# mLSTM, LRU and SSD steps at other beats, head squares tile by tile on POOL, and a tenth place for gated tiles

## The chip, the cores and the metric

The kernel runs on one core of a Trainium2 chip. It computes four layers in one launch on a sequence of 256 positions, in fp32. The metric is the device time of one execution in microseconds. The engines are named as in the profile: PE is TensorE, DVE is VectorE, ACT is ScalarE, POOL is GpSimd and SP is SyncE.

## What is computed

The reference applies two layers of a first block (LRU with mLSTM, then SSD) and two layers of a second one (attention with spatial gating, then a gated feed-forward net). The change touches the first block. Cut to its core:

```python
def lru_mlstm_layer(x, ...):
    u = x @ w_in                                   # 2048 -> 8192
    x_l, x_m, z = jnp.split(u, [LRU_WIDTH, LRU_WIDTH + MLSTM_WIDTH], axis=-1)
    y_l = rglru(causal_conv(x_l, ...), ...)        # 16 blocks of 128
    x_mc = jax.nn.silu(causal_conv(x_m, ...))
    q, k, v, o = ...                               # per head, 4 heads of 512
    gates = (gin @ w_if + b_if)                    # input and forget gate rows
    h = mlstm_chunkwise(q, k, v, ig, lf)
    h = rmsnorm(h, m_norm)                         # per head: sum of squares over 512
    y_m = (o * h).reshape(bn, s, MLSTM_WIDTH)
    y = jnp.concatenate([y_l, y_m], axis=-1) * jax.nn.silu(z)
    return y @ w_out

def ssd_layer(x, ...):
    z, xbc, dt = jnp.split(x @ w_in, ...)
    xbc = jax.nn.silu(causal_conv(xbc, ...))       # xs, B, C
    cb = einsum(cm, bm)                            # per group, 8 groups
    y = ssd_scan(xh, dt, a, bm, cm) + d_skip * xh  # 8 heads of 64 in a group
    y = y * jax.nn.silu(z)
    y = rmsnorm(y per group, gnorm)                # sum of squares over 512
    return y @ w_out
```

## The kernel before

Activations stand transposed, 128 features by 256 positions in a tile. Each weight matrix is read in chunks of 128 x 1024 (512 KB) by SP into RAW; ACT rounds a chunk to its high part WH, DVE subtracts to get the low part WL (line 1266, in RAW's place), and PE multiplies each 128 x 128 block twice: WL with the activation's high half (line 522, 256 columns) and WH with both halves (lines 521 and 524, 512 columns). An output tile (a job) sums 4 to 32 such blocks in one of four psG banks; ACT copies one half of the bank (`half`), DVE adds the other and scales (`evict`).

`Schedule` lists all jobs and cuts the chunks into 2324 beats, half a chunk each: four blocks, eight matmuls. Everything else is tied to beats. Each engine's program is one loop over the beats, and in each beat it issues the steps whose event lies a fixed number of beats back, `for h in at("head", b - 21)`, in the order in which the functions are called. Engines run free of each other otherwise and wait on semaphores: PE loops over beats with `lstm`, `norms`, `ssd` ahead of the beat's blocks; ACT splits a chunk at each even beat, three chunks ahead of PE, and DVE at each odd beat. So a step at a later beat stands behind more of the engine's own work; it takes no other time by itself. Jobs end at fixed beats: z tile n at 116 + 4n for n > 0, LRU tile n at 184 + 8n, LRU gate tile n at 180 + 8n, an SSD group every 40 beats.

**mLSTM.** Event `gates` is at beat 119; before the change `head` h is at 128 + 16h. The gate rows are made by ACT and DVE (`gates`), PE turns them to columns (line 587), ACT stores them and reads them back broadcast to NMB. For a head PE makes K Q products (594), DVE and ACT the weights E, PE the denominator (600) and four tiles of numerators (607), DVE scales them to hs (1413). POOL sums their squares into hacc (hq in the profile; `squares`, lines 1740 to 1746), PE sums them over partitions (`colsum`, line 505, head + 21), ACT makes the root hr in two activations (781, 783), DVE gates and scales hs with z tiles (1420 to 1423, semaphore h_y), ACT writes the high half to Y (yh_hi) and DVE the low half (yh_lo). z tiles are gated by ACT (993) and POOL (`fma`, lines 1725 and 1727, shared tile SQ); nine places hold them until their head is finished.

**LRU.** POOL convolves a tile (1730, 1725, 1727), PE multiplies by two 128 x 128 weights (617, 618), ACT and DVE make the gates, DVE scans and multiplies by the gate, ACT and DVE write Y. The last layer output reads Y of LRU tile 15 in beat 329.

**SSD.** For a group: convolutions of B, C and four x tiles, the product CB (642, event `cb`), eight heads of decay weights Et made by DVE (1528), ACT (exp) and DVE (1535, 1536) and used by PE (660, head event + 5), outputs gated by z on POOL (1819), squares summed on POOL (event `gsum`) and by PE (line 505 from sq, event `gnorm`), root on ACT, four normalising steps on DVE (1548), high half to Y on ACT, low half on DVE (1271).

## Time and profile before

| | before |
|---|---|
| median of 3 runs | 3592.89 us (3592.19 to 3593.06) |
| profiled execution, its own time | 3593.61 us |
| its span | 3591.7 us |
| granted TensorE clock over it | 0.991 |
| PE busy | 97% |
| DVE busy | 76% |
| ACT busy | 53% |
| POOL busy | 47% |
| HBM read | 618.75 MB, 173 GB/s |

The span runs from the first to the last instruction of the program; the time has some 2 us around it. Matmuls are pipelined, so a busy PE is not PE at its peak. In a timeline row the number in brackets is the time that the engine stood idle before the row, and what ended it; short ones are not printed. PEclk is the share of the full TensorE clock that was granted: 1.00 is 2.4 GHz, 0.50 is 1.2 GHz. The mLSTM heads stand between 217 and 381 us, the LRU tiles until 565, SSD from 720 to 1305.

### The profile page before, as it was taken

The page shows a single profiled execution, that of the slowest core. Times are in us where ns is not written, and L with a number is a line of the kernel's source. Part 1 is how long each engine was busy: PE and PEld are TensorE (multiplying, and loading weights), DVE is VectorE, ACT ScalarE, POOL GpSimd, SP SyncE. Part 2 cuts the span into 40 slices and gives each one's busy share as a digit, 9 for nine tenths or more (in the row PEclk, how much of TensorE's full clock was granted, in tenths as well). Part 3 has the DMA queues.
Part 4 walks back from the last instruction along what each step waited for, and adds up shares of the span by engine and source line. Part 5 has one row for each costly group of instructions (what it writes and reads, how often), then busy time and mean ns, then how long its engine had stood idle before and what let it go on. Part 6 is the DMA issues. An engine that isn't in the chain of part 4 may idle for free.

```text
span 3591.7 us, 52952 instructions
## 1 busy us (share of the span) xinstructions
PE 3489.6 (97%) x19584; PEld 3001.1 (84%) x19584; DVE 2729.6 (76%) x4035; ACT 1891.9 (53%) x2857; POOL 1689.4 (47%) x1473
## 2 busy tenths in 40 slices
PE   8998999999999999998999999999998999999999
PEld 7887788888887888886888888888886888888888
DVE  8768886679899976776788758877676788658875
ACT  6554785455555554765444434444765544434443
POOL 4324672167877822143366406653143466306640
PEclk9999999999999999999999999999998999999999
DMA  5544556655555556543555665566543555665566
GB/s 192 168 156 140 162 182 186 188 180 170 176 169 166 178 165 188 178 132 111 186 188 187 184 189 187 186 185 188 173 134 110 186 188 187 184 191 185 187 185 179
DMA packets 177041, 624.37 MB, mean 174 GB/s; under 512 B 19784, under 2 KB 25616, under 8 KB 175760
## 3 DMA queue, kind: packets, MB, share of 16 engines
q1 hardware_dynamic: 171216, 606.11, 53.7%
q10 hardware_dynamic: 5568, 14.89, 1.2%
q8 instruction: 155, 2.54, 0.3%
q14 instruction: 102, 0.84, 0.1%
HBM read 618.75 MB, written 2.17 MB: 173 GB/s over the span
## 4 chain that ended last, share of the span: by engine, by line
PE 71%; DVE 10%; POOL 5%; ACT 3%; issue 3%; DMA 0%; ACTq 0%; POOLq 0%; DVEq 0%
PE psG L524 43%; PE psG L522 23%; DVE WL L1266 3%; PE psG L521 2%; POOL SQ L1725 1%; ACT WH L761 1%; DVE sdx L1279 1%; POOL SQ L1744 1%; ACT L781 1%; POOL sdx L1727 1%; PE psM L547 1%; DVE Et L1528 1%; DVE Et L1535 0%; POOL GV L1866 0%; DVE Y L1271 0%
## 5 line engine op out<-in xcount | busy, mean ns | idle before, releaser
L524 PE MATMUL psG<-H,WH 128*128 128x512 f32 x5655 | 2025.9, 398 | 0.0
L1266 DVE TENSOR_TENSOR WL<-RAW,WH 128x1024 fp32r<-128x1024 f32 (+1 forms) x1162 | 1496.0, 1287 | 552.7 <-ACT WH L761 550.8
L761 ACT ACTIVATE WH<-RAW 128x1024 fp32r<-128x1024 f32 (+1 forms) x1162 | 1214.8, 1045 | 952.3 <-PE psG L524 932.5
L522 PE MATMUL psG<-H,WL 128*128 128x256 f32 x6032 | 1667.2, 287 | 0.1
L524 PEld LDWEIGHTS psG<-H,WH 128*128 128x128 f32 x5655 | 1068.5, 189 | 234.1
L522 PEld LDWEIGHTS psG<-H,WL 128*128 128x128 f32 x6032 | 1146.1, 190 | 45.3 <-issue 9.6
L524 PE MATMUL psG<-Y,WH 128*128 128x512 f32 x2816 | 998.6, 398 | 0.0
L522 PE MATMUL psG<-Y,WL 128*128 128x256 f32 x2944 | 807.5, 281 | 11.6 <-DVE Y L1273 10.6
L524 PEld LDWEIGHTS psG<-Y,WH 128*128 128x128 f32 x2816 | 530.4, 188 | 122.1
L522 PEld LDWEIGHTS psG<-Y,WL 128*128 128x128 f32 x2944 | 557.0, 189 | 26.0 <-DVE WL L1266 11.2
L1875 POOL TENSOR_SCALAR fou<-fsu,PAR 128x256 f32<-128x256 f32 x88 | 177.9, 2022 | 565.3 <-DVE fsu L1308 565.3
L1787 POOL TENSOR_TENSOR SQ<-X 128x256 f32<-128x256 f32 x75 | 49.5, 661 | 358.4 <-DVE X L1319 358.4
L1725 POOL TENSOR_SCALAR SQ<-fsu,PAR 128x255 f32<-128x255 f32 x176 | 172.8, 982 | 16.9
L1727 POOL TENSOR_TENSOR fou<-SQ,fou 128x255 f32<-128x255 f32 x176 | 166.5, 946 | 14.7
L521 PE MATMUL psG<-H,WH 128*128 128x512 f32 x377 | 154.9, 411 | 13.1 <-DVE H L1273 11.8
L1883 POOL TENSOR_TENSOR fou<-fou,fog 128x256 f32<-128x256 f32 x88 | 133.4, 1515 | 6.9
L1839 POOL TENSOR_TENSOR g_t<-g_s 128x256 f32<-128x256 f32 x32 | 48.2, 1505 | 182.6 <-DVE g_s L1308 182.6
L1725 POOL TENSOR_SCALAR SQ<-sds,PAR 128x255 f32<-128x255 f32 (+2 forms) x96 | 120.0, 1250 | 9.3
L1790 POOL TENSOR_TENSOR SS<-SS,SQ 128x256 f32<-128x256 f32 x75 | 119.0, 1587 | 5.9
L761 ACT ACTIVATE fsu<-psG 128x256 f32<-128x256 f32 x88 | 33.9, 385 | 153.3 <-PE psG L524 153.3
L761 ACT ACTIVATE fsg<-psG 128x256 f32<-128x256 f32 x88 | 33.8, 384 | 151.3 <-PE psG L524 151.1
L1295 DVE TENSOR_TENSOR fsg<-psG,fsg 128x256 f32<-128x256 f32 x88 | 37.4, 425 | 78.6 <-ACT fsg L761 78.5
(350 smaller groups left out, 3578.9 us busy)
## 6 DMA issues: line engine op xcount, KB each, us to landing
RAW<-in_w_up SPq DMA_DIRECT2D x352, 512.0 KB, 3.6
RAW<-in_w_o_in SPq DMA_DIRECT2D x162, 512.0 KB, 3.6
RAW<-in_w_e_in SPq DMA_DIRECT2D x128, 512.0 KB, 3.6
RAW<-in_w_down SPq DMA_DIRECT2D x128, 512.0 KB, 3.5
RAW<-in_w_in SPq DMA_DIRECT2D x112, 512.0 KB, 3.6
RAW<-in_w_o SPq DMA_DIRECT2D x72, 512.0 KB, 3.6
RAW<-in_w_e_out SPq DMA_DIRECT2D x64, 512.0 KB, 4.3
RAW<-in_w_o_out SPq DMA_DIRECT2D x64, 512.0 KB, 4.2
```

Of the source, the lines that this page charges most:

```text
L521: e.matmul(o, wh, x, start=True, stop=False)
L522: ins = e.matmul(o[:, 0:T], wl, x[:, 0:T], start=False, stop=False, skip_group_check=True)
L524: ins = e.matmul(o, wh, x, start=False, stop=last)
L761: copy = lambda o, i, scale=1.0: e.activation(o, i, ACT.Copy, scale=scale)
L1266: tt(WL_[c % NRAW][:, 0:n], RAW_[c % NRAW][:, 0:n], WH_[c % NW][:, 0:n].bitcast(F32), SUB).then_inc(sem("wl"), 1)
L1725: own.up(ts(m, a, s, None, op0))
L1727: return tt(o, m, c, op1)
L1787: own.up(tt(sq, X[n], X[n], MUL))
L1790: step(tt(ss, ss, sq, ADD), "ssq")
L1839: own.up(tt(t, s, s, MUL))
L1875: own.up(ts(o, s, par(key, "fw", 88 + n), par(key, "fb", n), MUL, ADD))
L1883: step(tt(o, o, f_og[p % 2], MUL), "f_mul")
```

## The change

Events move: `head` by two beats, `cb` by two, `gsum` by one and `gnorm` by two for the first seven groups. Steps of `gates` on PE and ACT and the whole LRU chain from PE's product on move by two or three beats. The squares of a head are summed tile by tile, the first at head + 12 and each next a beat later, where all four stood at head + 15. z tiles get a tenth place, which lies where a row of the gates stood, so tile 9 waits for the gate rows, and the wait for h_y starts with tile 10. DVE's write of hs waits for yh_lo in place of yh_hi.

```diff
@@ -251,16 +251,16 @@
     for h in range(4):
-        S.event("head", h, S.events[("gates", 0)] + 9 + 16 * h)
+        S.event("head", h, S.events[("gates", 0)] + 11 + 16 * h)
...
         x3 = S.end_of("sx", g * 4 + 3)
-        S.event("cb", g, S.end_of("sC", g) + 14)
+        S.event("cb", g, S.end_of("sC", g) + 16)
...
             S.event("shead", g * 8 + e, x3 + 12 + (4 if g < 7 else 2) * e)
-        S.event("gsum", g, x3 + (48 if g < 7 else 34))
-        S.event("gnorm", g, x3 + (55 if g < 7 else 35))
+        S.event("gsum", g, x3 + (49 if g < 7 else 34))
+        S.event("gnorm", g, x3 + (57 if g < 7 else 35))
@@ -351,7 +351,7 @@
     gs, ig, gf, gz, gG, gM, gon = slots("gg", 7, 36)
-    zb = slots("zb", 2, 43) + slots("zb_", 1, 22) + slots("zx", 6, 23)
+    zb = slots("zb", 2, 43) + slots("zb_", 1, 22) + slots("zx", 6, 23) + slots("zy", 1, 42)
@@ -451,7 +451,7 @@
 
-    PLACE = {"xm": (xm_s, 3), "z": (zb, 9), "zl": (lz, 4), "lru": (ls, 2), "sz": (sd_z, 4), "V": (v2, 2),
+    PLACE = {"xm": (xm_s, 3), "z": (zb, 10), "zl": (lz, 4), "lru": (ls, 2), "sz": (sd_z, 4), "V": (v2, 2),
@@ -580,7 +580,7 @@
                 ready(use, ins)
-            for _ in at("gates", b - 7):
+            for _ in at("gates", b - 9):
@@ -608,9 +608,9 @@
             for h in at("head", b - 21):
-                w.wait_ge(sem("h_ssq"), h + 1)
+                w.wait_ge(sem("h_ssq"), 4 * h + 4)
                 colsum(("hc", h), hacc)
-            for n in at("lru", b - 10):
+            for n in at("lru", b - 12):
@@ -812,7 +812,10 @@
                 if n >= 9:
-                    w.wait_ge(sem("h_y"), n - 8)
+                    w.wait_ge(sem("gate_rows"), 1)
+                if n >= 10:
+                    w.wait_ge(sem("h_y"), n - 9)
@@ -945,11 +948,11 @@
                 e.activation(gz[0:4, :], gz[0:4, :], ACT.Ln, bias=KC[0:4, 3:4]).then_inc(sem("gate_soft"), 1)
-            for _ in at("gates", b - 5):
+            for _ in at("gates", b - 8):
...
                 e.dma_start(scr_m[1], gG[0:4, :]).then_inc(sem("st_m1"), 16)
-            for _ in at("gates", b - 8):
+            for _ in at("gates", b - 10):
@@ -990,7 +993,7 @@
                 w.wait_ge(sem("z_act"), n - 1) if n > 1 else None
-                e.activation(zt[n % 2], zb[n % 9], ACT.Tanh, scale=0.5).then_inc(sem("z_tanh"), 1)
+                e.activation(zt[n % 2], zb[n % 10], ACT.Tanh, scale=0.5).then_inc(sem("z_tanh"), 1)
@@ -1001,14 +1004,14 @@
                 e.dma_start(LW[n % 4], I["w_lru"][n]).then_inc(sem(f"lw{n % 4}"), 16)
-            for n in at("lru", b - 11):
+            for n in at("lru", b - 13):
...
                 e.activation(i, use.ap[:, T:2 * T], ACT.Tanh, bias=halves[:, 16 + n:17 + n], scale=0.5).then_inc(use.sem, 1)
-            for n in at("lru", b - 13):
+            for n in at("lru", b - 15):
@@ -1017,10 +1020,10 @@
                 e.activation(r, r, ACT.Ln, bias=one_c).then_inc(sem("l_ln"), 1)
-            for n in at("lru", b - 16):
+            for n in at("lru", b - 18):
...
                 e.activation(lr[n % 2], lr[n % 2], ACT.Exp, scale=0.5).then_inc(sem("l_exp"), 1)
-            for n in at("lru", b - 19):
+            for n in at("lru", b - 21):
@@ -1409,7 +1412,7 @@
                     w.wait_ge(sem("small"), use.done)
-                    w.wait_ge(sem("yh_hi"), 4 * (h - 1) + i + 1) if h else None
+                    w.wait_ge(sem("yh_lo"), 4 * (h - 1) + i + 1) if h else None
@@ -1417,10 +1420,10 @@
                     w.wait_ge(sem("o_tanh"), n + 1)
-                    stt(zb[n % 9], Og[n], 1.0, zb[n % 9], ADD, MUL)
+                    stt(zb[n % 10], Og[n], 1.0, zb[n % 10], ADD, MUL)
...
                     w.wait_ge(own.sem, own.n)
-                    tt(hs[i], hs[i], zb[n % 9], MUL).then_inc(sem("h_y"), 1)
+                    tt(hs[i], hs[i], zb[n % 10], MUL).then_inc(sem("h_y"), 1)
@@ -1431,15 +1434,15 @@
                 stt(lz[n % 4], lt[n % 2], 1.0, lz[n % 4], ADD, MUL).then_inc(sem("lz_act"), 1)
-            for n in at("lru", b - 12):
+            for n in at("lru", b - 14):
...
                 stt(xc, i, 1.0, xc, ADD, MUL).then_inc(sem("l_gate"), 1)
-            for n in at("lru", b - 15):
+            for n in at("lru", b - 17):
...
                 tt(lr[n % 2], ll2[n % 2], lr[n % 2], SUB).then_inc(sem("l_dif"), 1)
-            for n in at("lru", b - 17):
+            for n in at("lru", b - 19):
@@ -1448,7 +1451,7 @@
                 tt(l2, l2, lz[n % 4], MUL).then_inc(sem("l_scan"), 1)
-            for n in at("lru", b - 20):
+            for n in at("lru", b - 22):
@@ -1762,11 +1765,20 @@
                 w.wait_ge(sem("z_tanh"), n + 1)
-                step(fma(zb[n % 9], zt[n % 2], 1.0, zb[n % 9], ADD, MUL), "z_act")
-            for h in at("head", b - 15):
-                w.wait_ge(small[("pn", h, 3)].sem, small[("pn", h, 3)].out)
-                w.wait_ge(sem("small"), small[("hc", h - 1)].done) if h else None
-                squares(hacc, hs, "h_ssq")
+                step(fma(zb[n % 10], zt[n % 2], 1.0, zb[n % 10], ADD, MUL), "z_act")
+            for i in range(4):
+                for h in at("head", b - 12 - i):
+                    w.wait_ge(small[("pn", h, i)].sem, small[("pn", h, i)].out)
+                    if i == 0:
+                        w.wait_ge(sem("small"), small[("hc", h - 1)].done) if h else None
+                        step(tt(hacc, hs[0], hs[0], MUL), "h_ssq")
+                    else:
+                        sq_free()
+                        own.up(tt(sq, hs[i], hs[i], MUL))
+                        w.wait_ge(own.sem, own.n)
+                        w.wait_ge(sem("h_ssq"), 4 * h + i)
+                        step(tt(hacc, hacc, sq, ADD), "h_ssq")
```

The rows below are the programs of an engine as built, in issue order: line, operation, tiles and shape. The changed kernel has the same statements some lines further on. First POOL in the mLSTM stage, head 1, before and then changed; hs are the head's four tiles, hq the sum, SQ and zt, zb, zx, zy belong to the gating of z.

```order
L1725 TENSOR_SCALAR SQ<-zt_140 128x256
L1727 TENSOR_TENSOR zb_132<-SQ,zb_132 128x256
L1740 TENSOR_TENSOR hq_122<-hs_118 128x256
L1744 TENSOR_TENSOR SQ<-hs_119 128x256
L1746 TENSOR_TENSOR hq_122<-hq_122,SQ 128x256
L1744 TENSOR_TENSOR SQ<-hs_120 128x256
L1746 TENSOR_TENSOR hq_122<-hq_122,SQ 128x256
L1744 TENSOR_TENSOR SQ<-hs_121 128x256
L1746 TENSOR_TENSOR hq_122<-hq_122,SQ 128x256
```

```order
L1775 TENSOR_TENSOR hq_122<-hs_118 128x256
L1728 TENSOR_SCALAR SQ<-zt_141 128x256
L1730 TENSOR_TENSOR zb_131<-SQ,zb_131 128x256
L1778 TENSOR_TENSOR SQ<-hs_119 128x256
L1781 TENSOR_TENSOR hq_122<-hq_122,SQ 128x256
L1778 TENSOR_TENSOR SQ<-hs_120 128x256
L1781 TENSOR_TENSOR hq_122<-hq_122,SQ 128x256
L1778 TENSOR_TENSOR SQ<-hs_121 128x256
L1781 TENSOR_TENSOR hq_122<-hq_122,SQ 128x256
```

The first square has moved ahead of a z tile's gating; the other six operations stay behind it.

Then DVE in the SSD stage where a group's outputs are normalised, before and then changed. Et are the weights of the next group's heads, sdx the outputs, sq the root, WL a weight chunk's low part.

```order
L1266 TENSOR_TENSOR WL_63<-RAW_62,WH_65 128x1024
L1548 SCALAR_TENSOR_TENSOR sdx_200<-sdx_200,gn_79,sq_211 128x256
L1548 SCALAR_TENSOR_TENSOR sdx_201<-sdx_201,gn_79,sq_211 128x256
L1535 SCALAR_TENSOR_TENSOR Et_186<-Et_186,ncs_188,CBt_182 128x256
L1536 SCALAR_TENSOR_TENSOR Et_186<-Et_186,ncs_188,CBt_182 128x128
L1548 SCALAR_TENSOR_TENSOR sdx_202<-sdx_202,gn_79,sq_211 128x256
L1548 SCALAR_TENSOR_TENSOR sdx_203<-sdx_203,gn_79,sq_211 128x256
L1266 TENSOR_TENSOR WL_53<-RAW_52,WH_66 128x1024
L1271 TENSOR_TENSOR Y<-sdx_200,Y 128x256
L1271 TENSOR_TENSOR Y<-sdx_201,Y 128x256
L1528 TENSOR_SCALAR Et_184<-csb,ncs_187 128x256
L1529 TENSOR_SCALAR Et_184<-csb,ncs_187 128x128
```

```order
L1269 TENSOR_TENSOR WL_63<-RAW_62,WH_65 128x1024
L1538 SCALAR_TENSOR_TENSOR Et_187<-Et_187,ncs_189,CBt_183 128x256
L1539 SCALAR_TENSOR_TENSOR Et_187<-Et_187,ncs_189,CBt_183 128x128
L1269 TENSOR_TENSOR WL_53<-RAW_52,WH_66 128x1024
L1551 SCALAR_TENSOR_TENSOR sdx_201<-sdx_201,gn_79,sq_212 128x256
L1551 SCALAR_TENSOR_TENSOR sdx_202<-sdx_202,gn_79,sq_212 128x256
L1531 TENSOR_SCALAR Et_185<-csb,ncs_188 128x256
L1532 TENSOR_SCALAR Et_185<-csb,ncs_188 128x128
L1551 SCALAR_TENSOR_TENSOR sdx_203<-sdx_203,gn_79,sq_212 128x256
L1551 SCALAR_TENSOR_TENSOR sdx_204<-sdx_204,gn_79,sq_212 128x256
L1298 TENSOR_TENSOR sds_190<-psG,sds_190 128x256
L1311 TENSOR_TENSOR sds_190<-sds_190,RS 128x256
```

The first normalising step, the one that waits for the root, has moved behind one pair of Et products and one WL; two steps on Et now stand between the normalising steps.

## Rows read from the trace of the kernel before

**Rows 1.** The page, busy time of each engine over the span.
```profile
PE 3489.6 (97%) x19584; PEld 3001.1 (84%) x19584; DVE 2729.6 (76%) x4035; ACT 1891.9 (53%) x2857; POOL 1689.4 (47%) x1473
```
**Rows 2.** PE's waits in 720 to 1310 us: total us, times, longest.
```profile
PE psM L660 <- DVE Et L1536: 6.2, 12, 0.5
PE psM L505 <- POOL sq L1746: 4.1, 6, 0.9
```
**Rows 3.** Timeline of PE, the four head sums: start, us, row, idle before.
```profile
262.13 0.48 PE L505 MATMUL psM<-hq,ONE 128*128 128x256 f32 x1
...
294.07 0.80 PE L505 MATMUL psM<-hq,ONE 128*128 128x256 f32 x1 [4.43 <-POOL hq L1746]
...
327.70 0.80 PE L505 MATMUL psM<-hq,ONE 128*128 128x256 f32 x1 [3.88 <-POOL hq L1746]
...
360.65 0.80 PE L505 MATMUL psM<-hq,ONE 128*128 128x256 f32 x1 [3.43 <-POOL hq L1746]
```
**Rows 4.** Timeline of PE, other single waits.
```profile
221.09 0.34 PE L587 MATMUL psM<-IDN,gg 4*128 4x4 f32 x2 [3.25 <-DVE gg L1382]
...
380.16 0.50 PE L521 MATMUL psG<-H,WH 128*128 128x512 f32 x1 [1.16 <-DVE WL L1266]
...
398.92 0.45 PE L617 MATMUL psM<-lxc,LW 128*128 128x256 f32 x1 [2.52 <-issue]
...
752.49 0.45 PE L642 MATMUL psM<-sdb,sdb 128*128 128x256 f32 x1 [1.92 <-DVE sdb L1500]
```
**Rows 5.** Windows: length, PE, PEld, DVE, ACT, POOL busy, PEclk, DMA share, GB/s.
```profile
221.09:227.19 6.10, 6.10 (x20) 5.21 (x21) 2.98 (x4) 1.73 (x5) 2.37 (x2) 0.50 0.02 5
262.13:289.64 27.51, 27.51 (x159) 24.15 (x158) 24.70 (x44) 16.70 (x29) 11.85 (x11) 1.00 0.50 162
294.07:298.87 4.80, 4.80 (x14) 4.11 (x15) 0.62 (x3) 0.90 (x1) 1.59 (x2) 0.50 0.01 2
294.07:323.82 29.75, 29.74 (x158) 25.93 (x158) 22.74 (x40) 15.70 (x25) 11.55 (x12) 0.92 0.43 136
327.70:333.00 5.30, 5.30 (x16) 4.54 (x17) 0.85 (x4) 1.38 (x2) 1.58 (x2) 0.50 0.08 15
360.65:363.72 3.07, 3.07 (x9) 2.60 (x10) 1.02 (x1) 1.59 (x3) 2.89 (x3) 0.50 0.00 0
380.16:396.40 16.24, 16.07 (x84) 12.89 (x84) 13.77 (x24) 13.92 (x24) 7.25 (x6) 1.00 0.50 165
400.00:500.00 100.00, 99.43 (x554) 85.25 (x553) 83.40 (x132) 86.46 (x139) 71.81 (x56) 1.00 0.56 177
600.00:700.00 100.00, 100.00 (x574) 87.11 (x573) 61.35 (x64) 42.79 (x45) 19.96 (x18) 1.00 0.60 188
752.84:756.25 3.41, 3.41 (x13) 2.93 (x12) 3.30 (x5) 0.00 (x0) 3.13 (x4) 0.50 0.18 70
```
**Rows 6.** Timeline of POOL, the gating ahead of head 1's squares, and the first square.
```profile
283.09 1.31 POOL L1725 TENSOR_SCALAR SQ<-zt 128x256 f32<-128x256 f32 x1 [5.26 <-ACT zt L993]
...
286.05 0.84 POOL L1740 TENSOR_TENSOR hq<-hs 128x256 f32<-128x256 f32 x1
```
**Rows 7.** Timeline of DVE in the period of head 1.
```profile
268.95 0.43 DVE L1420 SCALAR_TENSOR_TENSOR zb<-O__82,zb 128x256 f32<-128x256 f32 x1 [2.22 <-ACT hq L783]
...
280.35 0.41 DVE L1413 TENSOR_TENSOR hs<-psM,E 128x256 f32<-128x256 f32 x1
...
286.33 3.19 DVE L1266 TENSOR_TENSOR WL<-RAW,WH 128x1024 fp32r<-128x1024 f32 x2
```
**Rows 8.** Timeline of DVE, normalising of an SSD group and the next late Et.
```profile
920.27 0.88 DVE L1548 SCALAR_TENSOR_TENSOR sdx<-sdx,gn,sq 128x256 f32<-128x256 f32 x2 [2.29 <-ACT sq L783]
...
921.46 0.35 DVE L1536 SCALAR_TENSOR_TENSOR Et<-Et,ncs,CBt 128x128 f32<-128x128 f32 x1
...
922.66 1.21 DVE L1266 TENSOR_TENSOR WL<-RAW,WH 128x1024 fp32r<-128x1024 f32 x1
...
942.92 0.56 DVE L1536 SCALAR_TENSOR_TENSOR Et<-Et,ncs,CBt 128x128 f32<-128x128 f32 x1
```

## Prediction

> **What bounds the kernel.** I read the page first: TensorE is busy 97% of the span, VectorE 76% [rows 1]. So time is gained only where TensorE stands idle or runs at its lower clock, and the reader should look for its waits, not for totals of other engines. The list of TensorE's waits gives totals: in the SSD stage six sums over a group's squares (line 505 from sq) wait 4.1 us and twelve products wait 6.2 us for the weights Et, 0.5 each [rows 2]. TensorE's timeline says when the single long waits fall. The sums over a head's squares, heads 0 to 3, start at 262.13, 294.07, 327.70 and 360.65 [rows 3]; head 0 does not wait, the others wait 4.43, 3.88 and 3.43 us. Other single waits are 3.25 us for the gate rows, 1.16 for a low weight part WL, 2.52 at the first LRU product that waits (its releaser is not named; POOL's convolution ended just before) and 1.92 at the first CB product [rows 4].
>
> Behind five of these waits (the gate rows, heads 1 to 3, CB) TensorE's granted clock is 0.50, its 1.2 GHz level; in the five windows it works 22.68 us [rows 5]. The head period at full clock holds 27.51 us of work; the same period with 4.80 us at the lower clock takes 29.75. So a microsecond at the lower level costs 2.24/4.80 = 0.47, and all 22.68 cost 10.6. Waits of 1.16 and 2.52 us left the clock at 1.00 (the windows from 380.16 and from 400), one of 1.92 took it down: a wait of 1.2 has a row on its side, one of 2 us has one on either.
>
> A beat, the unit in which the change moves steps, is 8 matmuls. Undisturbed TensorE issues 574 in 100 us [rows 5], so a beat is 1.39 us and two are 2.79.
>
> **The change, part by part.** No arithmetic is added on any engine; only orders, waits and one buffer differ. All prices are against the profiled execution.
>
> 1. Gate rows. The transposes (line 587) go from beat 7 to 9 after the event. They start at 221.09 after a wait of 3.25, so they were due at 217.84, are due now at 220.63 and wait 0.46. That is 2.8 off, and the lower clock behind it (6.10 x 0.47) another 2.9. ScalarE's two stores of the rows move later in its program, yet waited for the same rows before, so their landing stays; the head's reads are two beats later too. **5.7.**
>
> 2. Sums of heads 1 and 2. All steps of a head move two beats together, so against each other nothing is gained; what changes is POOL. Before, POOL started head 1's seven square operations only after a z gating that stood ahead, at 286.05 [rows 6], and the sum started when they were done, at 294.07: 8.02 us, while it was due at 289.64. Now the first square stands ahead of that gating, and the other six follow it (the order rows). VectorE writes the first hs tile at 280.35 + 0.41, 18.6 us behind the previous sum [rows 7]. From there POOL needs its nine operations, at worst the 8.02 and the gating's 2.96 (283.09 to 286.05): it ends 29.6 after the previous sum, which is 2.1 late, since the next is due at 27.5. The other end is no wait, as head 0 has. I take 1.2, a little above the middle, since both later heads showed long squares. Two heads: 8.31 - 2.4 = 5.9, and the clock behind them, (4.80 + 5.30) x 0.47 = 4.7, because 1.2 is nearest to the wait of 1.16 that cost no clock. **10.6.** Head 0 had no wait and gets none.
>
> 3. Sum of head 3. Here z gating is over and POOL's first LRU convolution moves ahead of the squares with room, so the wait of 3.43 and its clock (3.07 x 0.47 = 1.4) go. But the WL behind it frees TensorE only at 380.16, 19.5 after the sum, where it was due at 379.00: between the root that VectorE waits for and this WL its timeline prints no idle time. With the clock up TensorE comes 1.4 earlier, and one product (0.4, as the 128x256 one at 280.35) moves ahead of VectorE's wait: the WL wait becomes 1.16 + 1.4 - 0.4 = 2.1. **4.8 - 1.0 = 3.8.** Ends: 1.16 stays, or 4 with the clock down.
>
> 4. LRU. The product moves two beats behind its convolution: the wait of 2.52 is below 2.79 and goes. In the steady part TensorE is busy 99.43 of 100 us [rows 5], over the 135 us to the last product another 0.8. **3.3.** At the end the last LRU tile is written in beat 326 in place of 324 and read in beat 329. VectorE, busy 83 of 100 us here, keeps up, so I cost that at nothing; without this cover it would be 2.8 once.
>
> 5. First CB product. Two beats later it is due at 753.36, and its tile was ready at 752.49. **1.9 + 3.41 x 0.47 = 3.5.**
>
> 6. SSD group sums. POOL's squares wait for data, not for a beat, so they end as before and the six waits (4.1) go. But the root, the eight normalising steps and VectorE's wait of 2.29 for that root [rows 8] move with the sum, 2.79 us nearer to an Et that was already 0.5 late. From 920.27 to that Et's end at 943.48 VectorE prints no pause: 23.2 us. Ahead of its wait it now does two Et products (921.15 to 921.81, 0.7) and one WL (1.1 before the next step), as the order rows show. So Et is late by 2.79 - 1.8 = 1.0 more; ScalarE has one copy less ahead of the root, which works against that, so the other end is none. I take the middle, 0.5, for each of six groups. **4.1 - 3.1 = 1.0.**
>
> 7. The tenth z place and its wait. ScalarE's copy of z tile 9 waited for head 0's first output; now tile 10 does, with two beats more room. The new wait is for the gate rows, there by 221.09. Waiting for yh_lo in place of yh_hi names VectorE's own earlier step. Behind these on ScalarE stand weight splits; three chunks of lead hide them. **0**, bounds -1 and +1.
>
> Sum: 5.7 + 10.6 + 3.8 + 3.3 + 3.5 + 1.0 = 27.9. The profiled execution took 3593.61 (span 3591.70); the median shown is 0.72 below. 3593.6 - 27.9 = 3565.7, as a median **3565 us**.
>
> Adding the good ends (heads 1 and 2 wait nothing +2.4, WL as before or gone +2.1, Et no later +3.1) gives -35.5. The bad ends (waits of 2.1 with the clock down: -1.8 - 4.7; WL at 4 with it: -3.3; Et 1.0 later: -3.0) give -15.
>
> **Rivals.**
> A. *Everything lands free*: 3593.6 - 35.5 = **3558**. For it: nearly each wait is shorter than the two beats. Against: POOL's nine operations and VectorE's full stretches.
>
> B. *VectorE becomes the bound.* It works 24.70 us in the 27.51 of a head period and waits 2.2 of the rest for the root [rows 5, 7]: nothing is left over. Beside POOL's squares two WL took 3.19 us, against 1.21 for one alone [rows 7, 8], +0.39 each. Should all nine POOL operations cost VectorE that, 3.5 us per period, TensorE would wait so three times, 10; the SSD gain of 1.0 and some of part 3 would go too: **3577**. Against: POOL does the same operations as before, and the first falls behind the WL with the least room. The Trainium skill, page "SBUF — State Buffer", section "Who interferes with whom", says that a VectorE instruction with two SBUF inputs and a GpSimd instruction that reads SBUF exclude each other for the whole instruction. By that rule each POOL operation of 0.6 to 1.6 us may hold VectorE for its length, and the sum would be this rival's rather than mine. The trace agrees that both slow down, but shows 0.39 per WL.
>
> C. *The waits only change places* (VectorE's lag is kept, and every microsecond TensorE gains is waited for at the next WL or Et): about **3592**, no change. Against: VectorE waits 2.22 for a head's root and 2.29 for a group's, so its lag ends there each time.
>
> D. *Slower.* The place is Et in the SSD stage: the normalising burst comes nearer, nothing is done ahead of it, and all twelve late Et reach the 1.92 us at which the clock fell. Each costs 1.4 more and 3 to 6 us at the lower clock (1.4 to 2.9): 12 x 3.6 = 43, against 31 gained elsewhere: **3605**. It decides from about 1.4 us of added lateness at both places; part 6 gives 1.0 at worst, at one of them.
>
> **How the numbers follow.** Forecast 0.62, A 0.14, B 0.15, C 0.05, D 0.04. Faster by over 0.2% (7 us, about what a measurement of this kernel can tell) is the first three, 0.91; within it 0.05; slower 0.04. The range takes in the forecast with its bounds, A with 3 us to spare, and B: 3555 to 3579.
>
> **What would show it.** Right: no wait at line 587 over 0.6; head sums waiting 0 to 2 us with a clock of 1.00 through 230 to 400; one WL wait of about 2 us behind the last head; no wait at the LRU and CB products; group sums without waits, Et waits of about 1 in their place. Wrong: the clock at 0.50 behind the head sums (B), Et waits of 2 us (D), or a TensorE wait of over 3 us at a place that had none. VectorE's busy time should stay within 1% of 2729.6 us.

## The result and the profile after

| | before | after |
|---|---|---|
| median | 3592.85 us (3592.19 to 3593.06, 4 runs) | 3576.70 us (3576.38 to 3578.97, 4 runs) |
| profiled execution | 3593.61 | 3576.60 |
| its span | 3591.7 | 3574.8 |
| granted TensorE clock | 0.991 | 0.995 |

The changed kernel takes 0.9957 of the time before (95% interval 0.9945 to 0.9969): faster, by 16.2 us in the medians and 17.0 in the profiled executions, where the forecast said 28. The time lies in the range and near rival B's 3577, so which steps held has to be read place by place. The page's row of busy times, against [rows 1]:

```profile
PE 3481.8 (97%) x19584; PEld 2996.2 (84%) x19584; DVE 2737.8 (77%) x4035; ACT 1889.9 (53%) x2857; POOL 1710.1 (48%) x1473
```

VectorE's busy time grew by 8 us, 0.3%. TensorE's waits over the whole span, three rows of the list (us in total, times, longest):

```profile
PE psM L660 <- DVE Et L1539: 12.9, 18, 1.5
...
PE psG L522 <- DVE WL L1269: 3.7, 3, 3.2
PE psM L505 <- POOL hq L1781: 3.3, 2, 1.7
```

The group sums no longer appear. The twelve Et waits of 6.2 us [rows 2] have become eighteen of 12.9. TensorE's timeline of the changed kernel, with the places of [rows 3] and [rows 4] (in brackets the idle time before a row and what ended it):

```profile
221.75 0.25 PE L587 MATMUL psM<-IDN,gg 4*128 4x4 f32 x2 [0.50 <-DVE gg L1385]
...
289.10 0.70 PE L505 MATMUL psM<-hq,ONE 128*128 128x256 f32 x2 [1.63 <-POOL hq L1781]
...
318.30 0.70 PE L505 MATMUL psM<-hq,ONE 128*128 128x256 f32 x2 [1.67 <-POOL hq L1781]
...
346.37 0.59 PE L505 MATMUL psM<-hq,ONE 128*128 128x256 f32 x2
...
355.45 0.67 PE L617 MATMUL psM<-lxc,LW 128*128 128x256 f32 x2 [1.53 <-issue]
...
368.15 0.43 PE L522 MATMUL psG<-H,WL 128*128 128x256 f32 x1 [3.17 <-DVE WL L1269]
...
924.34 0.65 PE L660 MATMUL psM<-Et,Xk 128*64 128x256 f32 x2 [1.48 <-DVE Et L1539]
...
938.75 0.62 PE L660 MATMUL psM<-Et,Xk 128*64 128x256 f32 x2 [0.50 <-DVE Et L1539]
```

The gate rows wait 0.50 in place of 3.25, heads 1 and 2 wait 1.63 and 1.67 in place of 4.43 and 3.88, head 3 not at all, and the CB product shows no wait. Against that stand an LRU product (355.45) and a WL (368.15) that wait longer than what stood there, and an Et of 1.48 in each group. The granted clock behind the sum of head 1 and behind the WL (windows: length; busy time of PE, PEld, DVE, ACT, POOL; PEclk; DMA share; GB/s):

```profile
289.10:294.50 5.40, 5.40 (x31) 4.78 (x32) 5.30 (x10) 4.40 (x9) 3.89 (x4) 1.00 0.32 98
...
368.15:375.00 6.85, 6.84 (x30) 5.96 (x31) 5.21 (x11) 5.52 (x10) 1.23 (x1) 0.75 0.17 50
```

The clock is at 1.00 behind the sum (behind head 2 as well) and falls behind the wait of 3.17, where before it fell behind the sums [rows 5] and stayed up behind the WL.

Where the time came from is read by the start of the same matmul of line 521 in both traces. The changed kernel's execution starts its steady work 0.6 us later, ahead of anything changed; from there:

| stretch | forecast | gained |
|---|---|---|
| gate rows (part 1) | 5.7 | 5.4 |
| sums of heads 1 and 2 (part 2) | 10.6 | 9.6 |
| sum of head 3 to the WL behind it (part 3) | 3.8 | 0.0 |
| LRU (part 4) | 3.3 | 2.9 |
| first CB product (part 5) | 3.5 | 3.8 |
| SSD groups (part 6) | 1.0 | -1.8 |
| attention and what follows | 0 | -2.4 |

These add up to 17.5; less the 0.6 of the later start they make 16.9. Single entries depend by some 0.2 on which matmul is taken. Three rows hold most of the miss: parts 3 and 6, and the last, where nothing was changed.

### The profile page after: what moved, and what is told of

It is laid out like the page before. It is cut to its first block, busy times and chain, and to the rows that moved or that the text cites. A ratio compares the mean times of both kernels' runs of the same rounds, so it can differ in the third digit from the quotient of the medians.

```text
span 3574.8 us, 52976 instructions
## 1 busy us (share of the span) xinstructions
PE 3481.8 (97%) x19584; PEld 2996.2 (84%) x19584; DVE 2737.8 (77%) x4035; ACT 1889.9 (53%) x2857; POOL 1710.1 (48%) x1473
## 4 chain that ended last, share of the span: by engine, by line
PE 80%; DVE 9%; ACT 4%; issue 3%; POOL 2%; DMA 0%; ACTq 0%; SPq 0%; DVEq 0%; POOLq 0%
PE psG L524 47%; PE psG L522 26%; PE psG L521 3%; DVE WL L1269 3%; ACT WH L761 1%; ACT L781 1%; PE psM L547 1%; DVE sdx L1282 1%; POOL SQ L1728 1%; PE psM L660 1%; POOL GV L1878 0%; PE psM L712 0%; DVE Et L1531 0%; DVE Y L1274 0%; ACT RL L781 0%
## 5 line engine op out<-in xcount | busy, mean ns | idle before, releaser
L522 PE MATMUL psG<-Y,WL 128*128 128x256 f32 x2944 | 808.4, 282 | 11.6 <-DVE Y L1276 10.6
L1728 POOL TENSOR_SCALAR SQ<-fsu,PAR 128x255 f32<-128x255 f32 x176 | 174.2, 990 | 16.9
L1728 POOL TENSOR_SCALAR SQ<-sds,PAR 128x255 f32<-128x255 f32 (+2 forms) x96 | 134.9, 1406 | 9.3
```

The source lines that it names most:

```text
L522: ins = e.matmul(o[:, 0:T], wl, x[:, 0:T], start=False, stop=False, skip_group_check=True)
L1728: own.up(ts(m, a, s, None, op0))
```

## The experiments

The kernel before ran beside each, on the same chip, with medians between 3591.2 and 3593.1; comparisons of medians below go by the difference to that (the changed kernel: -16.2). The 95% interval of each ratio reaches some 4.5 us to either side, and most of them overlap that of the changed kernel, so by the times alone differences of a few us to the changed kernel are not settled. A second measure is taken from the profiled executions: how much earlier or later the same matmuls of line 521 start than in the changed kernel, counted from the start of the steady work (near 195 us) to 1570 us, which is ahead of attention. The count from there matters, since the steady work itself starts at times up to 2.4 us apart, ahead of anything changed.

### Group sums back at the old beats

```diff
-        S.event("gsum", g, x3 + (49 if g < 7 else 34))
-        S.event("gnorm", g, x3 + (57 if g < 7 else 35))
+        S.event("gsum", g, x3 + (48 if g < 7 else 34))
+        S.event("gnorm", g, x3 + (55 if g < 7 else 35))
```

> The changed kernel with gsum and gnorm of the first seven SSD groups at their old beats (48 and 55). My theory: the two added beats cost more than they save, because the root and the eight normalising steps on VectorE come nearer to the next group's weights Et. In the changed kernel each of six groups has Et waits of 1.48, 0.50 and 0.17 where before had 0.66 (the sum) + 0.54 + 0.44. Undoing them should bring the six sum waits of about 0.7 back, the Et waits down to about 1.0 per group, and the time about 2 us below the changed kernel: 3574.7. Rival (part 6 of the prediction, a gain of 1.0): 1 us above it, 3577.7. Second rival: the loss in this stage has another cause, such as the cb event: the Et waits stay at 1.5 and the time is within 0.5 us of 3576.7 or above.

Measured: 3575.54 us (3572.30 to 3576.19), ratio 0.9951 (0.9938 to 0.9963), 17.0 under the kernel before: 0.8 better than the changed kernel, within what the medians can tell. The profiled execution is clearer: the same matmuls come 1.2 us earlier, all of it gained in the SSD stage. Its waits in 720 to 1310 us:

```profile
PE psM L660 <- DVE Et L1539: 5.8, 12, 0.5
PE psM L505 <- POOL sq L1749: 4.0, 6, 0.7
```

That is 9.8 us of waits for 12.9. The prediction's part 6 had the old beats as the slower ones; these are the faster by the starts of the matmuls.

### Head squares together again

```diff
-            for i in range(4):
-                for h in at("head", b - 12 - i):
...
+            for h in at("head", b - 15):
+                w.wait_ge(small[("pn", h, 3)].sem, small[("pn", h, 3)].out)
+                w.wait_ge(sem("small"), small[("hc", h - 1)].done) if h else None
+                squares(hacc, hs, "h_ssq")
```

> The changed kernel with the squares of a head again in one piece at head + 15. My theory (part 2): the sums of heads 1 and 2 wait about 4 us again in place of 1.6, both waits are followed by the half clock, head 3 waits about 3.4 at its sum: about 10 to 14 us more than the changed kernel, 3587 to 3591. Rival: the two waits shrank because the whole head moved by two beats against the z gating, and the order of the squares on POOL counts for nothing: sum waits stay at 1.6, time 3577.

Measured: 3581.70 us (3579.83 to 3582.87), ratio 0.9970 (0.9959 to 0.9981), 10.8 under the kernel before, so 5.4 worse than the changed kernel; by the same matmuls 3.4 later. It lies between the two expectations. The three sums in TensorE's timeline, and the window behind the first, with the clock at 1.00 (behind the second too; behind the third 3.41 us passed at 0.50):

```profile
289.38 0.70 PE L505 MATMUL psM<-hq,ONE 128*128 128x256 f32 x2 [2.62 <-POOL hq L1749]
...
319.59 0.70 PE L505 MATMUL psM<-hq,ONE 128*128 128x256 f32 x2 [2.68 <-POOL hq L1749]
...
351.42 0.70 PE L505 MATMUL psM<-hq,ONE 128*128 128x256 f32 x2 [3.71 <-POOL hq L1749]
```
```profile
289.38:294.00 4.62, 4.62 (x26) 4.09 (x27) 4.52 (x9) 3.65 (x7) 4.19 (x4) 1.00 0.26 85
```

POOL's timeline for head 1, first of this kernel, then of the changed one, shows why:

```profile
277.22 1.12 POOL L1728 TENSOR_SCALAR SQ<-zt 128x256 f32<-128x256 f32 x1 [6.57 <-ACT zt L996]
...
281.33 0.61 POOL L1743 TENSOR_TENSOR hq<-hs 128x256 f32<-128x256 f32 x1 [2.16 <-DVE hs L1416]
```
```profile
278.76 0.73 POOL L1775 TENSOR_TENSOR hq<-hs 128x256 f32<-128x256 f32 x1 [7.40 <-DVE hs L1416]
279.65 0.85 POOL L1728 TENSOR_SCALAR SQ<-zt 128x256 f32<-128x256 f32 x1 [0.16 <-POOL hq L1775]
...
287.46 1.59 POOL L1781 TENSOR_TENSOR hq<-hq,SQ 128x256 f32<-128x256 f32 x1
```

Before, POOL's gating held it from 283.09 until the first square at 286.05 [rows 6]. With heads two beats later that gating is over, and POOL idle for 2.16 us, when the first hs tile comes. So 1.8 of the 2.8 us off head 1's wait come from the event, 1.0 from summing tile by tile; for head 2 it is 1.2 of 2.2, and neither wait of 2.6 took the clock down. Head 3 is another case: its sum waits 3.71 with the squares together, 3.43 in the kernel before and nothing in the changed one, so there the tile-by-tile order did all of it.

### The LRU chain back

```diff
-            for n in at("lru", b - 12):
+            for n in at("lru", b - 10):
```

and the eight later steps of the chain two beats earlier likewise.

> The changed kernel with the LRU chain (PE's product and all that follows it) at its old distance of 10 beats. My theory: PE's product of tile 1 is due two beats earlier while POOL finishes its convolution at 355.4 us, behind the squares of head 3; a wait of about 4.3 us at line 617 with the half clock behind it in place of 1.53, then less at the WL behind head 3; in all 3 to 5 us more than the changed kernel: 3580 to 3582. Rival: the LRU chain is the reason why ScalarE makes the root of head 3 late (its Ln pair stands ahead of the root), so that two beats earlier the root and with it the WL come earlier, the WL wait of 3.17 falls under 2 and the time stays at or below 3576.7.

Measured: 3581.27 us (3579.90 to 3581.58), ratio 0.9968 (0.9955 to 0.9980), 11.3 under the kernel before: 4.9 worse than the changed kernel, and by the same matmuls 4.4 later. The product of tile 1 waits as my theory had it, a second LRU product waits 2.5, and the WL waits fall to 1.2 and 1.1:

```profile
354.09 1.19 PE L617 MATMUL psM<-lxc,LW 128*128 128x256 f32 x2 [3.43 <-issue]
```

### Without POOL's sums

```diff
-                        sq_free()
-                        own.up(tt(sq, hs[i], hs[i], MUL))
-                        w.wait_ge(own.sem, own.n)
                         w.wait_ge(sem("h_ssq"), 4 * h + i)
-                        step(tt(hacc, hacc, sq, ADD), "h_ssq")
+                        step(tt(hacc[:, 0:8], hs[i][:, 0:8], hs[i][:, 0:8], MUL), "h_ssq")
```

> The changed kernel with six of POOL's seven operations of a head's squares left out (the sum of squares then holds hs tile 0 alone in all but eight columns, so the root has wrong values; its time is what is asked). My theory for the missing gain behind head 3: POOL's squares both take POOL's time ahead of the convolution of LRU tile 1 and stretch VectorE's WL (3.31 us for two at 343.16). Without them: no wait at the sums of heads 1 and 2 (-3.3), none at line 617 (-1.5), the WL wait behind head 3 falls from 3.17 to about 1.5 and keeps the clock up (-1.7 - 1.6): -8, 3568.5. Rival: the root of head 3 is late through ScalarE's own order alone (it stands behind the Ln pair of an LRU tile, which waits for VectorE): WL wait stays at about 3.2 or grows by what is gained before it, and only 3 to 5 us are gained: 3572 to 3574.

This kernel leaves out six of POOL's seven operations on a head's squares; three products over eight columns stand in their place, so the sum holds the first tile alone.

Measured: 3570.38 us (3569.44 to 3572.65), ratio 0.9940 (0.9927 to 0.9952), 22.1 under the kernel before, 6.0 better than the changed kernel, and by the same matmuls 5.9 earlier. That is between the two expectations. The sums and the LRU product wait nothing, yet the WL waits more:

```profile
363.82 0.58 PE L522 MATMUL psG<-H,WL 128*128 128x256 f32 x1 [3.82 <-DVE WL L1269]
```

What lies between is a chain. In the changed kernel's timelines it runs over VectorE (the LRU gate, line 1441), ScalarE (which waits for it, loads tables for the Ln pair, 1021, and comes to the root, 781, behind a copy and a split) and VectorE again (the burst behind the root, 1423 first, and the WL):

```profile
348.85 0.41 DVE L1441 SCALAR_TENSOR_TENSOR lxc<-li,lxc 128x256 f32<-128x256 f32 x1
```
```profile
349.36 0.42 ACT L1017 ACTIVATE li<-lr 128x256 f32<-128x256 f32 x1 [1.52 <-DVE lxc L1441]
...
350.10 1.28 ACT L1021 ACT_TABLE_LOAD   x1
...
353.42 0.46 ACT L781 ACTIVATE RL<-psM,KC 128x256 f32<-128x256 f32 x1
```
```profile
355.64 0.52 DVE L1423 SCALAR_TENSOR_TENSOR zb<-O__82,zb 128x256 f32<-128x256 f32 x1 [0.86 <-ACT hq L783]
...
366.88 1.22 DVE L1269 TENSOR_TENSOR WL<-RAW,WH 128x1024 fp32r<-128x1024 f32 x1
```

From the gate's end at 349.26 to the WL's end at 368.10 are 18.8 us. In the run without POOL's sums the same two rows are

```profile
344.69 0.41 DVE L1441 SCALAR_TENSOR_TENSOR lxc<-li,lxc 128x256 f32<-128x256 f32 x1
...
362.55 1.22 DVE L1269 TENSOR_TENSOR WL<-RAW,WH 128x1024 fp32r<-128x1024 f32 x1
```

345.10 to 363.77: 18.7 us. In the kernel before the gate ended at 359.21 and the WL at 380.10, 20.9 us, of which ScalarE stood 2.0 waiting for TensorE, which stood at head 3's sum: 18.9 without it. So in this order of steps the chain has one length, and starts when VectorE reaches the gate; the runs with only SSD steps moved show 18.8 as well. What TensorE gains ahead of it returns as a wait at the WL, unless VectorE reaches the gate earlier too. Here it did so by 4.2 us, while TensorE came to its wait 5.0 earlier (360.00 for 364.98), and the wait grew by 0.65, about the difference.

### The root one beat earlier

```diff
-            for h in at("head", b - 22):
+            for h in at("head", b - 21):
                 w.wait_ge(sem("h_y"), 4 * h)
                 root(small[("hc", h)], hr, 1.0 / 512, sem("h_rms"))
```

> The changed kernel with ScalarE's root of each head at head + 21 in place of 22, so ahead of the Ln pair of an LRU tile and of one split. My theory for the missing gain behind head 3: the root ended at 355.61 us, 9 us behind its sum, because ScalarE had first the Ln pair, which waited for VectorE's gate, then a copy and a split. One beat earlier the root of head 3 should end near 350.5, VectorE's burst with the WL follows it, and the WL wait of 3.17 with its half clock goes or falls below 1: 3 to 5 us less, 3572 to 3574. Rival: VectorE is late by its own work (contention with POOL's squares and the convolution), so the WL comes at the same time and the wait stays at 2 to 3.2: 3576 to 3577.

Measured: 3581.41 us (3578.28 to 3582.77), ratio 0.9967 (0.9955 to 0.9980), 9.8 under the kernel before: 6.4 worse than the changed kernel by medians, 4.2 later by the same matmuls, and worse than both expectations. ScalarE behind head 3's sum, and the VectorE row that waits for it:

```profile
350.75 1.28 ACT L781 ACT_TABLE_LOAD   x1 [0.18 <-PE psM L505]
...
352.54 1.28 ACT L783 ACT_TABLE_LOAD   x1
...
354.88 1.28 ACT L1021 ACT_TABLE_LOAD   x1
...
356.99 0.36 ACT L761 ACTIVATE ls<-psG 128x256 f32<-128x256 f32 x1
```
```profile
357.46 0.42 DVE L1298 TENSOR_TENSOR ls<-psG,ls 128x256 f32<-128x256 f32 x1 [3.55 <-ACT ls L761]
```

In the changed kernel the root comes right behind the Ln pair with the copy between, and its Ln needs no table load of its own: two loads. Ahead of the pair it takes three, and the copy for VectorE stands behind them all. TensorE then waits 4.61 us for the WL, where it waited 1.53 and 3.17 at two places.

The time, though, was lost one head earlier: the same matmuls start 4.1 us late already ahead of head 3's sum, and 3.8 behind the WL of head 3. Behind head 2 no Ln pair stands near, and the root needs two loads in either kernel. But here too ScalarE's copy for VectorE stands behind the root, and VectorE idles 3.4 us for it; then TensorE waits for a WL, with 3.41 us at the clock of 0.50 behind it:

```profile
325.69 0.42 DVE L1298 TENSOR_TENSOR ls<-psG,ls 128x256 f32<-128x256 f32 x1 [3.39 <-ACT ls L761]
```
```profile
340.60 0.38 PE L522 MATMUL psG<-H,WL 128*128 128x256 f32 x1 [2.29 <-DVE WL L1269]
```

So the copy that falls behind the root explains the loss at head 2; the third load is at head 3, where no more was lost on balance.

### Group squares tile by tile, sum at beats 50, 52 and 54

```diff
+            for hd in at("shead", b - 8):
+                g, i = divmod(hd // 2, 4)
+                if hd % 2 and g < 7:
...
+                        step(tt(sacc, x, x, MUL), "s_ssq")
...
+                        own.up(tt(sq, x, x, MUL))
+                        w.wait_ge(own.sem, own.n)
+                        w.wait_ge(sem("s_ssq"), 4 * g + i)
+                        step(tt(sacc, sacc, sq, ADD), "s_ssq")
```

> The changed kernel with the squares of an SSD group summed tile by tile on POOL (a tile's right behind its gating), and PE's sum at beat 50 in place of 57. My theory: VectorE has its free time (1.0 and 1.25 us idle, before a full stretch of 23 us) ahead of the next group's Et, so a root and normalising steps seven beats earlier fall there; the six sums do not wait more than 0.5, the Et waits of 1.48 and 0.50 per group fall under 0.5 together: 9 to 13 us less in the stage, 3564 to 3568. Rival: the sum at beat 50 comes before POOL is done, waits 2 us or more in each of six groups and takes the clock down: 3580 or more.

> As the run before with PE's sum at beat 52. My theory: no sum waits, the Et waits lie a little above those at beat 50, since the steps fall nearer to Et: 3565 to 3570. If the sum at beat 50 comes too early (the rival there), this one is the faster by 6 us or more.

> The changed kernel with the squares of an SSD group summed tile by tile on POOL and PE's sum at beat 54. In the two runs before (beats 50 and 52) the sums waited 5.17 and 2.41 us, a difference of 2.76, one beat being 1.39 us, and the Et waits fell to one of 0.4 a group. My theory: POOL is done 2.41 us after beat 52, so the sum at beat 54 (2.8 later) waits nothing and keeps the clock up, and the Et waits stay under 1.0 a group, since VectorE's burst comes three beats earlier than in the changed kernel (2.15 a group there): 6 to 9 us less in the stage, 3568 to 3571. Rival (the burst cannot come nearer to Et without being paid for there, wherever it stands): Et waits of 1.5 to 2 a group, 3574 to 3577.

Measured: beat 50 gave 3618.08 us, ratio 1.0070 (1.0056 to 1.0084); beat 52 gave 3588.72, ratio 0.9990 (0.9981 to 0.9999); beat 54 gave 3575.61, ratio 0.9953 (0.9941 to 0.9966), 16.1 under the kernel before and so level with the changed kernel. By the same matmuls these are 41.0 later, 10.6 later and 2.1 earlier. TensorE's waits in 720 to 1310 us at beats 50, 52 and 54:

```profile
PE psM L505 <- POOL sq L1845: 36.1, 7, 5.2
...
PE psM L660 <- DVE Et L1539: 2.7, 7, 0.4
```
```profile
PE psM L505 <- POOL sq L1845: 16.8, 7, 2.4
PE psM L660 <- DVE Et L1539: 2.8, 7, 0.4
```
```profile
PE psM L660 <- DVE Et L1539: 11.2, 25, 0.7
```

A group waits 5.6, 2.8 and 1.8 us; with the squares in one piece 1.6 at beat 55 and 2.15 at 57. The rival at beat 50 was right, the theory at 52 (3565 to 3570) failed with it, and at 54 the rival was right again. There the sum is free, and Et takes up what it left. No beat of these frees both.

Which beat is best is not settled. The old one has the smallest sum of waits. But the rest of the stage, from a matmul behind the CB product (near 750 us) to one near 1325 us, took 578.2 us in the changed kernel, 576.7 with the old beats (576.4 in the kernel before) and 575.9 at beat 54, so by the starts of the matmuls the last is the shortest, by 0.8 us. The medians do not tell these two apart.

The two sums at 891.22 and 960.19 of the kernel with beat 52 waited 2.41 and 2.42 us. The windows behind them:

```profile
891.22:894.63 3.41, 3.41 (x22) 3.10 (x23) 3.02 (x6) 3.25 (x4) 2.35 (x2) 1.00 0.08 31
961.10:964.50 3.40, 3.40 (x17) 3.03 (x15) 2.26 (x4) 3.21 (x4) 1.56 (x2) 0.51 0.07 29
```

One wait kept the clock, the other did not, behind the same work of the same loop. Of the seven waits of this kind in this execution two were followed by the clock at 0.50.

### The CB event back

```diff
-        S.event("cb", g, S.end_of("sC", g) + 16)
+        S.event("cb", g, S.end_of("sC", g) + 14)
```

> The changed kernel with the event of the CB product at its old beat (14 behind the end of C). My theory (part 5): the first CB product waits 1.9 us again with 3.4 us of half clock, or 1.9 alone: 1.9 to 3.5 more than the changed kernel, 3578.6 to 3580.2. Rival: the time gained there is waited for again at the next Et or WL of the first group, or the Et waits of all groups are the worse for the two beats: the same time or less, 3574 to 3577.

Measured: 3579.32 us (3577.70 to 3581.89), ratio 0.9964 (0.9952 to 0.9977), 11.9 under the kernel before, 4.3 worse than the changed kernel; by the same matmuls 2.2 were lost at this product, and 1.7 remained at 1570 us. The product waits again, with the clock at 1.00 behind it in the profiled execution, where before it was 0.50 behind a wait of 1.92 [rows 4, 5]:

```profile
736.30 0.67 PE L642 MATMUL psM<-sdb,sdb 128*128 128x256 f32 x2 [1.91 <-DVE sdb L1503]
```

### LRU tile 0 back, the other tiles later, and gating on POOL

The first two have the group sums tile by tile at beat 54, the third the old group beats. All change the LRU distances:

```diff
-            for n in at("lru", b - 12):
+            for n in [n for n in at("lru", b - 10) if n == 0] + [n for n in at("lru", b - 12) if n > 0]:
```

and so in the eight other places. The second has `b - 13` for the tiles above 0, and the third, with that, takes four products off VectorE:

```diff
+            for h in at("head", b - 9):
+                if h == 3:
+                    for n in range(12, 16):
+                        w.wait_ge(sem("z_act"), n + 1)
+                        w.wait_ge(sem("o_tanh"), n + 1)
+                        step(fma(zb[n % 10], Og[n], 1.0, zb[n % 10], ADD, MUL), "h_g")
```

> As the run before, with the chain of LRU tile 0 alone two beats earlier (as before the change), so that ScalarE's wait for VectorE's gate and its Ln pair stand clear of the root of head 3. Theory 1 (the root of head 3, and behind it the WL, is late because ScalarE stands 1.5 us at the Ln pair waiting for VectorE): the root ends 1 to 3 us earlier against its sum (9.0 us in the changed kernel), and the WL wait of 3.17 falls to 0 to 2, with the clock up: 2 to 4 us below the run before. Theory 2 (VectorE is simply full from the hs tiles of head 3 to this WL, and the order on ScalarE only shifts who is named): the WL wait with the smaller ones around it stays within 1 us, and the time within 1 us of the run before.

> As the run before, with the chain of all other LRU tiles one beat later. The product of tile 1 waited 1.53 us for POOL's convolution in the changed kernel; one beat is 1.39. Theory: this wait goes to 0.1 to 0.3, but under theory 2 of the run before, the WL wait behind head 3 takes up what is gained here: the sum of both within 1 us. Under theory 1 a further 1.4 us less. The last LRU tile is written one beat later, two beats ahead of its use: no cost, or a wait of at most 1.4.

> The LRU order of the run with tile 0 back and the rest later, the SSD group sums as before the change (beats 48 and 55), and one new thing: for head 3 the four products of z tiles with the output gate (0.42 us each on VectorE, behind the root) are made by POOL ahead of the squares, where POOL stood idle 8.5 us. In the four orders tried so far TensorE's waits between 335 and 385 us add up to 5.3 to 5.7 us, whatever stands where. Theory 2 (VectorE is full there, its work is the bound): taking 1.7 us of it away takes 1.5 to 2.5 us from that sum, which falls to 3 to 4, and if the longest wait falls under 2 the half clock goes too, 1.6 to 3.2 more. Rival (the sum is set by ScalarE's root, 9 us behind the sum over partitions, or POOL's extra four steps slow VectorE by as much as it saves): the waits stay at 5 or more. With the group stage of the old beats (1.5 us under the changed kernel's) the whole is 3568 to 3571 by theory 2, 3572 to 3574 by the rival.

Measured: 3574.98 us, ratio 0.9955 (0.9942 to 0.9967); 3572.54 us (3572.29 to 3574.72), ratio 0.9950 (0.9936 to 0.9963); 3574.49 us (3573.51 to 3575.43), ratio 0.9947 (0.9934 to 0.9961). They lie 16.7, 19.1 and 18.6 under the kernel before; by the same matmuls they are 1.0, 3.7 and 2.0 ahead of the changed kernel, where the run with beat 54 alone is 2.1 ahead; so moving tile 0 back cost 1.1. TensorE's waits from 335 to 390 us add up to 5.2 in the changed kernel, then 5.7, 5.5 and 6.3; with the LRU chain back, above, 8.9, and with the early root 7.1. The waits of the third:

```profile
340.42 0.48 PE L617 MATMUL psM<-lxc,LW 128*128 128x256 f32 x1 [2.21 <-DVE hs L1416]
...
365.65 0.50 PE L521 MATMUL psG<-H,WH 128*128 128x512 f32 x1 [3.06 <-DVE WL L1269]
```

Theory 1 of the first run falls: the WL wait stays at 3.2. The rival of the last run holds, and its trace shows both of its reasons. While POOL made the four products, VectorE took 10.3 us from a WL (329.68) to its first hs tile (339.95), for which it took 8.7 in the run before (328.21 to 336.91): 1.6 given back ahead of the 1.7 saved. And the root came no earlier:

```profile
356.56 1.28 ACT L781 ACT_TABLE_LOAD   x1
...
358.35 1.28 ACT L783 ACT_TABLE_LOAD   x1
```

With the pair of tile 0 earlier, a z tile's Tanh falls between pair and root, and the root has to load its own tables. VectorE stood idle 2.0 us for it. So theory 2 as I put it, a VectorE that is full, is not right for this last piece either; a chain through both engines fits. It is not the one of 18.8 us any more: in these three runs the WL ends 17.0, 17.0 and 16.0 us behind the same gate, and the root 11.5 behind the sum over partitions, where the changed kernel has 9.2.

What the second run gained over the first, 2.8 us by the same matmuls, is elsewhere. The windows of 400 to 560 us, first of the changed kernel, then of the second run:

```profile
400.00:560.00 160.00, 159.42 (x891) 137.23 (x891) 138.93 (x201) 134.29 (x210) 108.24 (x81) 1.00 0.58 181
```
```profile
400.00:560.00 160.00, 160.00 (x904) 139.23 (x904) 136.47 (x203) 135.27 (x212) 95.68 (x81) 1.00 0.58 184
```

Thirteen more matmuls at 0.17 us are 2.3 us; the first run, with 889 matmuls, is fifteen behind, 2.6 us. In that run most LRU products waited 0.10 to 0.12 us for their convolution, 1.4 in all; in the changed kernel they waited 0.6 in all, and with one beat more nothing. The waits alone do not fill the gain in either case, and what the rest is stays open. Against the changed kernel the second run had lost part of this before: it waited 4.12 us for the WL behind head 3, with 6.83 us at the clock of 0.50 behind it, and by the end of the LRU tiles it was ahead by only 0.7. Most of its lead, 2.9 us, comes from the SSD stage with the group squares summed tile by tile. By its median it is the fastest of the kernels that compute the whole result, but the intervals of the last three runs, of beat 54 and of the old group beats overlap. The same with the old group beats was run only together with the gating on POOL.

## Why the prediction was right, and where it was not

The gain of 16.2 us is well short of the 28 that were forecast. The range takes it in because its slow end was set by the bad bounds and by rival B; that the time lies beside B's is luck for B, as said below, and no merit of the middle value.

**Parts 1, 2, 4 and 5 held**, 21.7 us gained for 23.1 forecast. The gate rows wait 0.50 (said: 0.46). The working of part 2 stands: from POOL's first square to the sum 10.3 us, said at worst 11.0; the wait was 1.6 for 1.2. The clock stayed up. What its reason got wrong is the share of tile-by-tile summing at these two heads, 1.0 us of the 2.8 and 2.2 taken off the waits, not the whole; the event did the rest. And since waits of 2.62 and 2.68 kept the clock in one run, a wait near 1.2 was not needed for it. Part 5's 3.8 is the wait of 1.92 and the clock behind it; with the event back 2.2 were lost, the wait without the clock. The distances of the gate rows (part 1) and the tenth z place with its waits (part 7) were not undone by themselves: part 1 is read from the timeline, and part 7's nothing was not tested.

**Part 3 failed** at "the WL behind it frees TensorE only at 380.16, 19.5 after the sum": the wait of 3.43 at the sum and its clock went, as forecast, but the WL did not come earlier by as much. I tied the WL to the sum, over a timeline without idle time between root and WL. It is tied to VectorE's LRU gate, 18.8 us ahead, since ScalarE's Ln pair and with it the root wait for that; the run without POOL's sums shows it, where the gate came 4.2 us earlier than in the changed kernel, the WL 4.3 and the sum 3.3. The sum came 14.3 us earlier, and the WL 12.0: 21.8 behind it. So the wait was 3.17 in place of 2.1, and took the clock down, which was the bad bound. The LRU product of tile 1 (1.53) was not seen: in the kernel before TensorE's wait at head 3's sum had covered POOL's convolution behind the squares. With the squares together again the sum waits 3.71 and this product nothing. Removing a wait uncovers all that it hid, not only the next row.

**Part 6 failed** on a size. The wait at the late Et went from 0.5 to 1.48, which is the "1.0 more" that the text gives as the worst end, and I took the middle, 0.5, for a ScalarE copy; the worst end came, so the copy brought nothing that the trace shows. A second Et added 0.17. By the lists of waits the six groups lost 6.7 us at Et for 4.1 saved at the sums, 2.6; the starts of matmuls show 1.8.

**Attention**, in no part. The waits of this stage agree (the longest, for gq, is 5.13 and 5.14), but not the clock. Windows around it, before and after:

```profile
1624.00:1644.00 20.00, 14.87 (x75) 12.65 (x74) 15.64 (x26) 12.05 (x25) 8.78 (x10) 0.91 0.27 86
```
```profile
1605.00:1625.00 20.00, 14.86 (x66) 12.43 (x65) 15.64 (x26) 10.57 (x23) 7.89 (x9) 0.83 0.26 82
```

Nine matmuls fewer in the same busy time: the lower clock lasted 6.83 us in place of 3.41, which is 1.6 us by the prediction's price. The other traces do not make this chance: at this place all twelve runs have 6.83 us as the changed kernel has, and only the one trace of the kernel before has 3.41. All thirteen lose 1.5 to 2.9 us against it between its 1597 and 1721 us. Nor does the clock alone explain it: the changed kernel stood 17.1 us at 0.50 in that stretch and lost 2.2, the run with the old group beats 20.5 and lost 1.5, and in the second attention stage (from 2600 us) the kernel before has 20.5 and the changed one 17.1 with no gain. Whether the changes bring this loss, or the one trace before was a lucky one, stays open.

**The rivals.** A falls with the two sums that still wait 1.6 and the WL that waits 3.17. B came nearest in time but not by its mechanism: TensorE did not wait three times for VectorE behind head sums at a lower clock. C is right in one stretch of two: at head 3, waits only changed places. D was the right place, with Et waits of 1.5 once a group, and never reached the point where it decides.

## What to carry to other kernels

When a step is moved earlier or a wait taken out, look for the chain that sets the next operand's time through all engines, back to where it starts, not for the event that stood nearest before it: here 18.7 to 18.9 us of VectorE, ScalarE and VectorE again kept their length as long as the order of the steps stayed, whatever TensorE gained ahead of them. Where an engine fills a burst ahead of a deadline, price the loss at the worst end and try the burst's place at several beats; of five tried here, two lay within 1 us of each other and three were worse. Compare profiles by the same instructions from a common start: the sum of waits ranked those two the other way round. And count the small waits in the steady part: one more beat for the LRU tiles gave 2.8 us between two runs, while the moves around the last long wait gave nothing on balance.

## What was unexpected of the hardware

The length of a wait does not by itself decide about the clock. Two waits of 2.41 and 2.42 us in the same loop gave 1.00 and 0.51; waits of 2.62 and 2.68 kept 1.00, while 1.92 once lost it and 1.91 once did not. Over all fourteen traces, between 200 and 1330 us, TensorE waited 16 times for 1.9 to 2.7 us, and 0.50 went with four of these waits; it went with all 24 waits of over 3 us.

VectorE is slowed by POOL more than part B's 0.39 per WL: the same 14 instructions took 10.3 us with POOL busy beside them and 8.7 with POOL idle. Over 720 to 1310 us, summing group squares tile by tile raised VectorE's busy time too, from 518.3 in the changed kernel to 529.4 us at beat 54, with 837 instructions for 835, though POOL's own busy time fell from 438.1 to 419.9:

```profile
720.00:1310.00 590.00, 577.19 (x3201) 477.21 (x3200) 529.37 (x837) 313.09 (x493) 419.88 (x379) 1.00 0.54 172
```

By the Trainium skill's rule as the prediction cites it ("SBUF — State Buffer", "Who interferes with whom"), POOL's eight operations for those four products, 7.3 us of its time, could have held VectorE as long; they cost it 1.6, and a price is better taken from such a pair of runs.
